# Split value products in the second phase, and q and k transposed whole before they are split in the first

## What is computed

```python
def sb_block(q, q_pos, k, v, k_pos):
    z = jnp.einsum('bqhd,bkhd->bhqk', q, k) * SB_HD ** -0.5
    mask = (k_pos[None, :] < q_pos[:, None])[None, None]
    log_beta = jax.nn.log_sigmoid(z)
    l = jnp.where(mask, jax.nn.log_sigmoid(-z), 0.0)
    c = lax.cumsum(l, axis=3, reverse=True) - l
    w = jnp.where(mask, jnp.exp(log_beta + c), 0.0)
    return jnp.einsum('bhqk,bkhd->bqhd', w, v)
```

## Time and profile before

| | |
|---|---|
| median of 3 runs | 3234.82 us (3234.36 to 3235.14) |
| the profiled execution, its own time | 3235.57 us |
| its span, first to last instruction | 3233.5 us |
| busy: PE, DVE, ACT, POOL | 3104.9, 1905.3, 1732.7, 1102.1 us |
| mean granted TensorE clock | 0.979 of 2.4 GHz |
| moved by DMA | 400.69 MB |

### The profile page before, as it was taken

One profiled execution on the slowest core, in us unless ns is written; L12 is line 12 of the kernel. 1 busy time (PEld: TensorE's weight loads), 2 busy tenths in 40 slices (PEclk: granted clock), 3 DMA queues, 4 the chain that ended last, 5 costly groups with the idle time before them and its releaser, 6 DMA issues. The chain is left out here.

```text
span 3233.5 us, 49170 instructions
## 1 busy us (share of the span) xinstructions
PE 3104.9 (96%) x18410; PEld 2669.8 (83%) x18410; DVE 1905.3 (59%) x3388; ACT 1732.7 (54%) x3224; POOL 1102.1 (34%) x642
## 2 busy tenths in 40 slices
PE   6999999999769998999999999999999999999999
PEld 5778787877669998888888988888898888888998
DVE  2565656556446665666666777776756676653333
ACT  3544534444357764655555666666646555543443
POOL 0231414214135662333223322222332332334665
PEclk9999999999869999999999999999999999999999
DMA  4554544444364554232333422222252333334443
GB/s 149 176 165 146 181 131 146 154 130 126 116 183 139 175 166 154 72 101 85 111 94 119 126 80 87 87 89 89 88 179 84 107 98 110 96 98 140 130 134 117
DMA packets 309565, 400.69 MB, mean 124 GB/s; under 512 B 69249, under 2 KB 223890, under 8 KB 308306
## 3 DMA queue, kind: packets, MB, share of 16 engines
q1 hardware_dynamic: 309330, 397.55, 39.2%
HBM read 339.95 MB, written 57.54 MB: 123 GB/s over the span
## 5 line engine op out<-in xcount | busy, mean ns | idle before, releaser
L1847 POOL TENSOR_TENSOR st_ul<-st_ur,st_uh 128x1024 fp32r<-128x1024 f32 x180 | 430.5, 2413 | 766.1 <-ACT st_uh L1655 766.1
L1854 POOL TENSOR_TENSOR st_dl<-st_dr,st_dh 128x1024 fp32r<-128x1024 f32 x180 | 427.5, 2397 | 686.3 <-ACT st_dh L1665 686.3
L1821 DVE TENSOR_TENSOR st_ya<-st_ya,st_dp 128x512 f32<-128x512 f32 x544 | 368.7, 680 | 102.0 <-PE st_dp L1575 100.5
L1622 ACT ACTIVATE st_a<-st_z 128x512 f32<-128x512 f32 (+3 forms) x336 | 177.0, 527 | 395.9 <-PE st_z L1434 261.6
L1747 DVE TENSOR_TENSOR_SCAN st_g<-st_z,st_g,st_a 128x511 f32<-128x511 f32 (+3 forms) x336 | 370.9, 1104 | 16.0 <-DVE st_g L1740 0.8
L1808 DVE TENSOR_TENSOR st_tl<-st_dp,st_th 128x512 fp32r<-128x512 f32 (+2 forms) x168 | 96.8, 576 | 440.7 <-ACT st_dp L1703 440.6
L1457 PEld LDWEIGHTS st_po<-st_v,st_wt 128*128 128x128 f32 x2256 | 303.6, 195 | 41.2 <-DMA st_v<-out_new_v 19.0
L1575 PE MATMUL st_dp<-st_dh,st_tl 128*128 128x512 f32 x1020 | 336.7, 401 | 0.0
L1575 PE MATMUL st_dp<-st_dh,st_th 128*128 128x512 f32 x1020 | 336.0, 401 | 0.6 <-DVE st_ya L1821 0.6
L1575 PE MATMUL st_dp<-st_dl,st_th 128*128 128x512 f32 x1020 | 335.2, 400 | 0.0
L492 PE MATMUL fr_pj<-fr_wl,fr_xh 128*128 128x512 f32 x816 | 329.9, 404 | 0.0
(11 more groups left out here) (166 smaller groups left out, 5845.2 us busy)
## 6 DMA issues: line engine op xcount, KB each, us to landing
st_ur<-in_w_up SPq DMA_DIRECT2D x75, 1024.0 KB, 5.4
st_dr<-in_w_down SPq DMA_DIRECT2D x75, 1024.0 KB, 4.9
fr_wr<-in_w_in SPq DMA_DIRECT2D x96, 512.0 KB, 4.0
k_t<-fr_stT SPq DMA_DIRECT2D x21, 512.0 KB, 4.2
st_ur<-in_w_out SPq DMA_DIRECT2D x10, 1024.0 KB, 5.7
st_dr<-in_w_out SPq DMA_DIRECT2D x10, 1024.0 KB, 6.2
fr_xb<-in_x SPq DMA_DIRECT2D x17, 512.0 KB, 5.0
q_t<-fr_stT SPq DMA_DIRECT2D x17, 512.0 KB, 4.9
```

Of the source, the lines that this page charges most:

```text
L1821: dve.tensor_tensor(part, part, dp[:, k % BANKS], ALU.add).then_inc(s_fd, 1)
L1847: pool.tensor_tensor(ul[:, c], ur[:, c], raw(uh[:, c]), ALU.subtract).then_inc(s_ul, 1)
L1854: pool.tensor_tensor(dl[:, k], dr[:, k], raw(dh[:, k]), ALU.subtract).then_inc(s_dl, 1)
```

## The change

- **Phase 1, q and k.** `item_halves` and the old `item_rests` are gone. The finished item in `nq` is transposed whole: two heads, 128 columns, make one transpose, 4 an item, in one bank of `tt`, planned 8200 ns after the slot. ACT copies the bank to the high half `sth`, DVE subtracts from the bank to `stl` and frees it. Four DMAs of 64 partitions store the item where one did.
- **Phase 1, values.** Each SB_V bank is, after the copy to `ng`, also split into `vst` (ACT and DVE, which now frees the bank), and stored to a new DRAM tensor `vs`. Four cached value tiles are loaded and split too.
- **Phase 2.** ACT writes the high half of the transposed weights (`wth`), DVE the rest (`wtl`), both in part 1, the first ahead of `weights`. A value product is two float32r matmuls: `wth` with the tile's 128 columns (64 high, 64 low), then `wtl` with the 64 high ones. The result has two halves of 64 columns, which DVE adds (a copy and an addition in part 2, ahead of the scan); ACT's `output` is gone. Value tiles come from `vs` in packets of 512 bytes.

```diff
         for s in self.items:
-            tt += [Use(self.item_at(s) + 11000 + a, ("t", self.item[s], 0, a), "A") for a in range(2)]
+            if s[0] != "w":
+                tt.append(Use(self.item_at(s) + 8200, ("t", self.item[s], 0, 0), "D"))
...
                     elif kind == "t":
-                        pe.wait_ge(s_ql, b + 1)
+                        if b < NI:
+                            pe.wait_ge(s_ck[b], 16)
+                        else:
+                            pe.wait_ge(s_qg, b - NI + 1)
                         for h in range(4):
-                            mm = pe.transpose(bank[:, h * P:(h + 1) * P], raw(stk[:, b % 2, 4 * a + h]).rearrange("p a d -> p (a d)"), idt[:])
+                            mm = pe.transpose(bank[:, h * P:(h + 1) * P], nq[:, b % 2, h * P:(h + 1) * P], idt[:])
...
-                    sp.dma_start(dst.rearrange("h p k -> p h k"), raw(stT[:, c % 2])).then_inc(s_sd[c % 2], 16)
+                    dst = dst.rearrange("(a e) (i p) k -> e i p a k", e=2, i=2)
+                    for e in range(2):
+                        for i, part in enumerate((sth, stl)):
+                            sp.dma_start(dst[e, i], raw(part[64 * e:64 * e + 64, item_buffer(c)])).then_inc(s_sd[item_buffer(c)], 16)
...
+                    act.activation(sth[:, n % 2], tt[:, plan.tt.bank("t", c, 0, 0)].rearrange("p (h k) -> p h k", k=P), ACT.Copy).then_inc(s_qh, 1)
...
+                    dve.tensor_tensor(stl[:, n % 2], tt[:, plan.tt.bank("t", c, 0, 0)].rearrange("p (h k) -> p h k", k=P),
+                                      raw(sth[:, n % 2]), ALU.subtract).then_inc(s_ttd, 1)
...
                 for c in range(un.n):
-                    mm = pe.matmul(po[:, tt % 2 * HD:(tt % 2 + 1) * HD], wt[:, u % 3, c * P:(c + 1) * P],
-                                   v[:, p, un.e * jobs[un.job].keys + un.lo + c],
-                                   start=(un.first and c == 0), stop=(un.last and c == un.n - 1))
+                    tile = v[:, p, un.e * jobs[un.job].keys + un.lo + c]
+                    pe.matmul(out, wth[:, u % 3, c * P:(c + 1) * P], tile.rearrange("p i d -> p (i d)"), start=(un.first and c == 0), stop=False)
+                    mm = pe.matmul(out[:, 0:HD], wtl[:, u % 3, c * P:(c + 1) * P], tile[:, 0], start=False, stop=(un.last and c == un.n - 1))
...
+            def transposed_high(u):
+                n = units[u].n * P
+                act.wait_ge(s_tr, u + 1)
+                if u >= 3:
+                    act.wait_ge(s_pv, u - 2)
+                act.activation(wth[:, u % 3, 0:n], tp[:, 0:n], ACT.Copy).then_inc(s_wh, 1)
...
             def part1(u):
+                if u(2) is not None:
+                    transposed_high(u(2))
                 if u(1) is not None:
                     weights(u(1))
...
-            def transposed(u):
+            def transposed_low(u):
                 n = units[u].n * P
-                dve.wait_ge(s_tr, u + 1)
-                if u >= 3:
-                    dve.wait_ge(s_pv, u - 2)
-                dve.tensor_copy(wt[:, u % 3, 0:n], tp[:, 0:n]).then_inc(s_wt, 1)
+                dve.wait_ge(s_wh, u + 1)
+                dve.tensor_tensor(wtl[:, u % 3, 0:n], tp[:, 0:n], raw(wth[:, u % 3, 0:n]), ALU.subtract).then_inc(s_wt, 1)
...
+                    dve.tensor_copy(dst, po[:, tt % 2, HD:2 * HD]).then_inc(s_oc, 1)
+                    dve.wait_ge(s_oc, tt + 1)
+                    dve.tensor_tensor(dst, dst, po[:, tt % 2, 0:HD], ALU.add).then_inc(s_of, 1)
```

More of the change, by code:

```diff
@@ L165, in __init__ @@
         self.end_all = len(self.slots) * SLOT
-        self.items = [("c", t) for t in range(NC)] + [s for s in self.slots if s[1] in (SB_Q, SB_K)]
+        self.items = [(kind, t) for t in range(NC) for kind in "cw"] + [s for s in self.slots if s[1] in (SB_Q, SB_K)]
         self.item = {s: c for c, s in enumerate(self.items)}
@@ L318, in kept_done, with item_buffer, consumed @@
             eng.wait_ge(s_ngd[q % 2], 16 * (q // 2 + 1))
+        columns = [c for c, s in enumerate(plan.items) if s[0] != "w"]
+        def item_buffer(c):
+            return columns.index(c) % 2
+        def consumed(eng, c):
+            if plan.items[c][0] == "w":
+                eng.wait_ge(s_vl, plan.items[c][1] + 1)
+            else:
+                eng.wait_ge(s_tt, plan.tt.full("t", c, 0, 0))
         def x_at(t):
@@ L393, in key_stores @@
                 for s in plan.items:
-                    if s[1] == SB_K and s[0] != "c":
+                    if s[1] == SB_K and s[0] not in ("c", "w"):
                         b, g, j = s
@@ L698, in evacuations @@
                         slot_done(act, s)
[L699 to L710, removed]
@@ L712, in item_columns @@
-            def item_columns():
[L713 to L720, removed]
+                        act.activation(ng[:, q % 2], bank, ACT.Copy).then_inc(s_vc if g == SB_V else s_pja, 1)
@@ L836, in item_sums @@
             def item_sums():
-                for s in plan.items[NC:]:
-                    r = plan.item[s] - NC
+                for s in plan.items[NI:]:
+                    r = plan.item[s] - NI
                     yield plan.end(*s) + 800
@@ L1713, in part2 @@
             def part2(u):
-                if u(3) is not None:
-                    output(u(3))
                 if u(-1) is not None:
@@ L1823, in part0 @@
             def part0(u):
-                if u(2) is not None:
-                    transposed(u(2))
+                pass
             def part1(u):
@@ L1829, in part1 @@
                     negated_softplus(u(0))
+                if u(2) is not None:
+                    transposed_low(u(2))
             def part2(u):
+                if u(3) is not None:
+                    output(u(3))
                 if u(0) is not None:
```

171 lines of the change are left out of this document (110 added, 61 removed).

## The result

The changed kernel takes 3335.8 us (3332.6 to 3345.5, 4 runs) against 3234.6 for the kernel before on the same chip (3233.9 to 3235.1): a ratio of 1.032, interval 1.0295 to 1.0341. The forecast was 3239, with a range up to 3266. The profiled execution took 3332.64 us, span 3330.9, mean granted clock 0.971 (0.979 before).

The account below looks back on a forecast made before the run. PE, busy 96% of the span, was taken as the bound, except in phase 2's block 0. Terms -16.6 - 2.5 + 9 + 1 + 0 + 6 + 2 + 5 = +3.9 gave 3239 us, range 3216 to 3266.

Parts of the forecast that it names:

- The transposes, -16.6 and -2.5: Phase 1 on PE: 152 of 304 transposes go, -16.6 us; waits behind `fr_stk` go with the operation, -2.5 us.
- The place, +9: Phase 1: transposes of q and k come earlier and wait for POOL's gain; seven late items, 16.2 us, taken as +9.
- Other work of phase 1, at nothing: Phase 1: added ACT and DVE work and 139 more DMAs issued by SP lie behind PE and cost nothing.
- The value product, nothing: Phase 2 on PE: two float32r products take 0.22 us a tile, like one float32 product; 2256 records stay.
- ACT and DVE in blocks 1 to 4 and the passages, +8: Phase 2: added ACT and DVE work mostly hidden, +6 us in blocks 1 to 4, +2 for passages between blocks.
- third rival: Phase 2: high half ahead of `weights`, or later release of `tp`, makes PE wait in blocks 2 to 4; 3260, chance 0.15.
- Block 0, +5: First 16 units of phase 2, where the chain is the bound: high half and output addition cost +5 us, between 0 and 12.
- phase 1's end, +1: End of phase 1: the last value tile needs one more ACT copy, one subtraction and a store, +1 us.
- second rival: Phase 1: the late chain gains what ACT no longer holds in front of it; some 3 us of new waits, 3221, chance 0.22.
- two passes: Value product on PE: the trace shows a float32 product as two passes, each no dearer than a float32r one.

Follow-up runs that it names:

- e8: Kernel before with only q, k and cached k transposed whole, at the old place 11000 ns after the slot, four stores an item: 3212.5 us, 0.9933.
- e4: Changed kernel with the transposes of q and k planned 11000 ns after their slot in place of 8200: 3317.0 us, 1.0258.
- e10: Kernel before with whole transposes alone, those of q and k at the early place, 8200 ns: 3231.6 us, 0.9993.
- e13: e10 with an item's four stores planned 2800 ns later, to stand behind the load of the third pair of weights: 3227.8 us, 0.9973.
- e5: Changed kernel with cached value tiles loaded into two buffers of their own, planned earlier: 3324.2 us, 1.0278.
- e9: Changed kernel with one-column subtraction as tensor_scalar, both weight halves in part 0, q and k transposes at 11000 ns, own cached-value buffers: 3232.7 us, 0.9995.
- e11: e9 with PE leaving out the second value product of each tile, so the output lacks that term: 3124.6 us, 0.9661 to the kernel before.
- e3: Changed kernel with the one-column subtraction ssum - a written as a tensor_scalar, its place in the order unchanged: 3281.5 us, 1.0148.
- e1: Changed kernel's phase 1 with phase 2 as in the kernel before: 3258.8 us, 1.0076.
- e7: Changed kernel with the one-column subtraction as tensor_scalar and both halves of the transposed weights in part 0 of the step: 3274.3 us, 1.0121.

## Why the prediction was wrong, step by step

- **The transposes, -16.6 and -2.5: right.** e8 shows 22 to 23, with an interval of 16 to 27.
- **The place, +9: too small by half.** e4 and e10 give 19. The late items were found, and rightly put at the third tiles: seven with 16.2 us forecast, six with 18.4 measured, the worst 7.13, not 3.53. The failure is in what was taken off the 16.2. I took ends of gains from the trace of before as if the chain ahead of them stayed. It got later: the four stores went ahead of the third load, 7.4 us of waits (e13). The step names them, at some 0.4 us each, and still goes down from there; in this trace one takes 0.62 to issue (median of 152), and up to 1.66. "Less about one us at each" had the wrong sign. The bounds, 0 to 22, hold the 19. Nor had the sum any term for the clock behind a wait.
- **Other work of phase 1, at nothing: wrong.** ACT "under 55% busy" said nothing of order. A load that shares a buffer with k's items comes late, ACT waits for it in order, and what PE needs stands behind: 22 us in slots 9 to 15, of which 15 go with buffers of their own (e5). The prediction named the cover, PE's lag, but never asked what stands behind each added wait on ACT. By medians the transposes (-22), the place (+19) and these buffers (+12) add up to 9 of phase 1's 24 us. Of the 15 that are left, 11 are the two losses feeding each other (e9); the rest stays open.
- **The value product, nothing: right.** 2256 records in both, and four tiles take 0.81 us from their first product to the next dense one (2020.54 to 2021.35), as before (2006.48 to 2007.29); in place a product is worth 0.096 (e11).

```profile
2020.54 0.22 PE L1512 MATMUL st_po<-st_v,st_wth 128*128 128x128 f32 x1
...
2021.27 0.24 PE L1513 MATMUL st_po<-st_v,st_wtl 128*128 128x64 f32 x1
2021.35 0.47 PE L1629 MATMUL st_dp<-st_dh,st_th 128*128 128x512 f32 x1
```

- **ACT and DVE in blocks 1 to 4 and the passages, +8: the step that failed.** Measured 73: PE waited 60.6 us for the release of `tp`, which the term had as nearly hidden. The third rival was the true case, with "later release of `tp`" as its mechanism, and the test named for it (PE idle over 15 us in blocks 2 to 4) was met; its price of 27 was too small. The term's upper bound was also cut short: 22 is one unit in three late by 0.59 in block 3 alone (112 units), while the term is for blocks 1 to 4 (320 units), where the same rate gives 63. The row for it stood in the trace of before, the maximum of 2364 ns beside a median of 160 at a 128x1 instruction, and the change put the release of `tp` behind it. Without that instruction's hold the same work costs 23 (e3 against e1: 3281.5 - 3258.8), well placed 15.5 (e7), block 0 included, where the prediction had 0 to 22, 2 and 0 to 12. So the bounds were wide enough for the work and wrong for the order.
- **Block 0, +5, and phase 1's end, +1: of the right size.** The stretch took 54.77 against 51.85, 2.9 more, and phase 2 starts 21.0 us late where phase 1's last matmul is 20.3 late.
- **The range** ended 6 us above the third rival's price, taken alone. Two losses at once, 24 in phase 1 and 77 in phase 2, weren't in it. The second rival's sum also leaves out the terms +1, +2 and +5; with them it would be -5, 3230, not 3221.

## What to carry to other kernels

When a step moves behind another on its engine, look up the longest duration of what now stands ahead, not its median; a tiny instruction can hold the queue for as long as another engine's large one. For each wait that an edit adds, list what is queued behind it on that engine and who waits for that, since busy shares don't show it. And split a change: here the 152 transposes alone, at the old place, gained 0.7%, and the rest of the edit hid it.

## What the hardware showed

- **DVE held by POOL.** A tensor_tensor on one column with both inputs in SBUF took 0.16 us, and up to 2.4 while POOL subtracts 128x1024; the same arithmetic as a tensor_scalar with the second operand as scalar took 0.212 to 0.218 in all 200 cases (e3). Wider ones are held as well: in the changed kernel two of the 17 scalar_tensor_tensors of 128x1024 with both inputs in SBUF (L1857) took 3.3 us, beside POOL's instructions, where the rest took 1.27 to 1.48.
- **Small products cost alike.** A float32r product of 64 columns and one of 128 both took 0.11, and a float32 product of 64 columns twice that. The Trainium skill, TensorE: Matmul & The Clock Gate, section LDWEIGHTS (loading the stationary operand), has a formula for the load of a stationary operand that goes by its columns alone, by which 128 columns would be an estimated 128 / 1.2 = 107 ns; 0.11 from the rows agrees, and 0.096 in place (e11) is a little under it. The Trainium skill, FP8 and Floating Point Precision, section TensorE Precision Notes, has four passes for true FP32; the kernel before has two records for each of its 1128 products and pays 0.20 to 0.22 us for one, the price of two float32r products. What happens inside a record no run shows, so the price at this size is settled and the number of passes is not; the prediction's "two passes" says more than its rows.
- **A wait costs more than itself, or less.** After 7.13 us without PE the granted clock was 0.50 for some 8 us. Removing 41 us of waits gave 54 (e3); removing 7.4 gave 3.8 by medians and 6 by ratios (e13).
